# Eight of twelve modulation pieces beside the inverse go to ScalarE and GpSimd, and TensorE sums their partitions

## The reference

```
mod = c_act @ w_ada[l] + b_ada[l]                  # block 1, 6 x 1024 outputs
mod = silu(c) @ ada_w[i, j] + ada_b[i, j]          # block 2, four times 3 x 1024 outputs
q, k, v = causal_conv_silu(h @ w_in ...)           # mixer of block 1
o_dn = chunk_gated_delta_rule(q, k, v, g, beta)    # chunks of 64 tokens, 4 heads
o_sw = sliding_window_attention(...)
x = x + gate1 * (concat(o_dn, o_sw) @ w_out)
```

## Time and profile before

| | |
|---|---|
| median of 3 runs | 2992.44 us (2991.61 to 2999.63) |
| profiled execution, own time | 2987.68 us |
| its span | 2986.0 us |
| mean granted clock of TensorE | 0.961 of full speed |
| busy: TensorE, VectorE, ScalarE, GpSimd | 92%, 38%, 16%, 8% of the span |
| first projection begins | 38 us |
| pieces 20 and 21 | from 258.6 us |
| inverse, slots 0 to 19 | 262.8 to 361.2 us |
| products with k and recurrence | 361.2 to 404.7 us |
| attention | 404.7 to 448 us |
| product with `w_out` | from 451.4 us |

### The profile page before, as it was taken

One profiled execution on the slowest core, in us unless ns is written; L12 is line 12 of the kernel. 1 busy time (PEld: TensorE's weight loads), 2 busy tenths in 40 slices (PEclk: granted clock), 3 DMA queues, 4 the chain that ended last, 5 costly groups with the idle time before them and its releaser, 6 DMA issues.

```text
span 2986.0 us, 37205 instructions
## 1 busy us (share of the span) xinstructions
PE 2748.3 (92%) x15695; PEld 1353.8 (45%) x15695; DVE 1139.2 (38%) x1423; ACT 465.3 (16%) x916; POOL 238.3 (8%) x364
## 2 busy tenths in 40 slices
PE   7988989698899989999995999999999999999998
PEld 3446765232223322232332465477554334546763
DVE  3865453411111111121123254454536663344544
ACT  1122042000000000000000143000013662200001
POOL 1000011011111001101011500000000110000000
PEclk9988989799999999999997999999999999999999
DMA  9776411889999999999999112132223223221310
GB/s 338 282 254 231 179 30 48 315 344 407 401 381 397 409 406 407 409 406 400 413 409 367 38 59 90 57 113 79 90 59 71 58 64 113 106 85 57 112 57 28
DMA packets 170833, 639.49 MB, mean 214 GB/s; under 512 B 75907, under 2 KB 77531, under 8 KB 138129
## 3 DMA queue, kind: packets, MB, share of 16 engines
q1 hardware_dynamic: 156818, 607.76, 53.2%
q0 software_dynamic: 13792, 29.39, 3.4%
q10 hardware_dynamic: 64, 0.07, 0.0%
HBM read 626.44 MB, written 15.23 MB: 215 GB/s over the span
## 4 chain that ended last, share of the span: by engine, by line
PE 50%; issue 33%; DMA 5%; DVE 5%; POOL 3%; POOLq 2%; ACT 2%; DVEq 1%; SPq 0%; ACTq 0%
PE ps L2442 10%; PE ps L2477 10%; PE ps L2780 4%; PE ps L2513 4%; PE ps L2157 3%; DMA slots<-in_ada_w_dram 2%; PE ps L3036 2%; PE ps L2407 2%; PE ps L2324 2%; PE ps L2427 2%; PE ps L1221 2%; POOLq L1677 2%; DMA slots<-in_w_ada_dram 2%; PE ps L2796 1%; POOL work L1686 1%
## 5 line engine op out<-in xcount | busy, mean ns | idle before, releaser
L1787 PE MATMUL ps<-slots,hT 128*32 128x512 f32 x5120 | 564.6, 599 | 13.5 <-DMA slots<-in_w_up_dram 12.4
L1787 PEld LDWEIGHTS ps<-slots,hT 128*32 128x32 f32 x5120 | 165.6, 111 | 387.7 <-issue 365.0
L2477 PE MATMUL ps<-slots,work 128*128 128x512 f32 x672 | 289.6, 592 | 2.8 <-DVE work L2555 2.8
L1825 PE MATMUL ps<-slots,work 128*32 128x512 f32 x2112 | 247.8, 613 | 48.0 <-DMA slots<-in_w_down_dram 46.1
L1939 DVE TENSOR_SCALAR stage<-ps 128x512 f32<-128x512 f32 (+1 forms) x47 | 32.2, 686 | 548.8 <-PE ps L1791 548.4
L2477 PEld LDWEIGHTS ps<-slots,work 128*128 128x128 f32 x672 | 127.5, 190 | 162.5 <-issue 157.8
L2442 PE MATMUL ps<-hT,slots 128*128 128x256 f32 x768 | 168.7, 379 | 0.0
L1825 PEld LDWEIGHTS ps<-slots,work 128*32 128x32 f32 x2112 | 69.9, 112 | 196.3 <-issue 191.0
L2780 PE MATMUL ps<-hT,slots 128*128 128x512 f32 x352 | 156.6, 601 | 0.0
L2442 PEld LDWEIGHTS ps<-hT,slots 128*128 128x128 f32 x768 | 145.9, 190 | 22.4 <-issue 2.9
L2652 DVE TENSOR_TENSOR work<-work,ps 128x1024 f32<-128x1024 f32 x60 | 71.6, 1218 | 165.2 <-PE ps L2477 164.9
(11 more groups left out here) (587 smaller groups left out, 3431.2 us busy)
## 6 DMA issues: line engine op xcount, KB each, us to landing
slots<-in_w_up_dram SPq DMA_DIRECT2D x128, 2048.0 KB, 20.3
slots<-in_w_down_dram SPq DMA_DIRECT2D x64, 2048.0 KB
slots<-in_mlp_w_dram SPq DMA_DIRECT2D x32, 2048.0 KB, 7.9
slots<-in_ada_w_dram SPq DMA_DIRECT2D x40, 1024.0 KB, 4.9
slots<-in_w_ada_dram SPq DMA_DIRECT2D x16, 1024.0 KB, 5.6
slots<-in_w_in_dram SPq DMA_DIRECT2D x5, 2048.0 KB, 15.7
slots<-in_rnn_w_in_dram SPq DMA_DIRECT2D x24, 384.0 KB, 4.2
slots<-in_w_ada_dram SPq DMA_DIRECT2D x4, 2048.0 KB, 12.6
```

Of the source, the lines that this page charges most:

```text
L1787: ins = pe.matmul(to, x[:, k, unit * UNIT:(unit + 1) * UNIT], upw[s][:, k % 2, col:col + CH], start=k == 0, stop=False)
L1825: ins = pe.matmul(to, actT[:, 4 * q + j, 64 * u + 32 * h:64 * u + 32 * h + 32], downw[sl[h]][:, j, half * CH:(half + 1) * CH], start=k == ...
L2477: ins = pe.matmul(ps[:, bank + t], x[:, k, t * P:(t + 1) * P], w[:, k], start=k == 0, stop=k == HK - 1)
```

## The change

Group 5 stays with TensorE, and its pieces now stand ahead of slot 0 (20 and 21), in slot 1 (22) and in slot 2 (23). Groups 6 and 7 become 16 units of 1 MB (128 rows of 2048 columns). SyncE loads them through the two halves of slot 4; unit h waits until unit h - 2 has been summed. ScalarE multiplies a unit in place by its column of `cT` (`pool_scale`), GpSimd adds it to an accumulator in slot 5 in two instructions of 1024 columns (`pool_sum`; for the first unit of a group they are copies), and TensorE sums over the partitions and adds the bias as it does for the side groups: group 6 in slot 18, group 7 behind the recurrence. Which columns belong to groups 5, 6 and 7 is exchanged, and the bias rows are loaded to match. `w_out` is loaded when slot 4 and slot 5 have been read for the last time. The wait for the stored modulations moves from ScalarE to GpSimd. The semaphore `c_silu` is renamed `c_made` and also counts the scaled units.

```diff
+        POOL_FIRST = 6
+        POOL_UNITS = (N_ADA - POOL_FIRST) * KT
+        POOL_BEFORE = 5
...
-            if g < 6:
-                return [(w2v[g - 2], 0, 4 * CH, A2 + (g - 2) * 3 * D)]
-            return [(w2v[l], 4 * CH, HALF, A2 + l * 3 * D + 4 * CH) for l in (2 * (g - 6), 2 * (g - 6) + 1)]
+            if g < 5 or g == 6:
+                l = 3 if g == 6 else g - 2
+                return [(w2v[l], 0, 4 * CH, A2 + l * 3 * D)]
+            return [(w2v[l], 4 * CH, HALF, A2 + l * 3 * D + 4 * CH) for l in ((2, 3) if g == 5 else (0, 1))]
...
@@ ada_bias_loads
-                g.dma_start(dst[2:6], b2v[:, half * D:(half + 1) * D]).then_inc(S("dnw_in"), 16)
-                g.dma_start(dst[6:8], b2v[:, 2 * D:3 * D].rearrange("(g h) n -> g h n", h=2)[:, half]).then_inc(S("dnw_in"), 16)
+                g.dma_start(dst[2:5], b2v[0:3, half * D:(half + 1) * D]).then_inc(S("dnw_in"), 16)
+                g.dma_start(dst[5:6], b2v[2 + half:3 + half, 2 * D:3 * D]).then_inc(S("dnw_in"), 16)
+                g.dma_start(dst[6:7], b2v[3:4, half * D:(half + 1) * D]).then_inc(S("dnw_in"), 16)
+                g.dma_start(dst[7:8], b2v[half:half + 1, 2 * D:3 * D]).then_inc(S("dnw_in"), 16)
...
@@ ada_sp
-            for n in range(N_SIDE, 4 * N_ADA):
+            for n in range(N_SIDE, 4 * POOL_FIRST):
...
+            for h in range(POOL_UNITS):
+                g, k = POOL_FIRST + h // KT, h % KT
+                if h < 2:
+                    sp.wait_ge(freed[4], loads[4])
+                else:
+                    sp.wait_ge(S("side_free"), N_SIDE + h - 1)
+                dst, src = ada_slots[:, 4, h % 2], w2v[3, k * P:(k + 1) * P, 0:4 * CH]
+                if g == 7:
+                    dst, src = dst.rearrange("p (l n) -> p l n", l=2), w2v[0:2, k * P:(k + 1) * P, 4 * CH:4 * CH + HALF].rearrange("l p n -> p l n")
+                sp.dma_start(dst, src).then_inc((landed[4], S("side_in"))[h % 2], 16)
+
+        def pool_part(h):
+            return ada_slots[:, 4, h % 2].rearrange("p (j n) -> p j n", j=4)
+
+        def pool_scale(a, h):
+            k = h % KT
+            if h % 2 == 0:
+                a.wait_ge(landed[4], 16 * (POOL_BEFORE + h // 2 + 1))
+            else:
+                a.wait_ge(S("side_in"), 16 * (N_SIDE + h // 2 + 1))
+            a.activation(pool_part(h), pool_part(h), ACT.Copy, scale=cT[:, 1, k:k + 1]).then_inc(S("c_made"), 1)
+
+        def pool_sum(pool, g):
+            acc = side_acc(g)
+            for k in range(KT):
+                h = (g - POOL_FIRST) * KT + k
+                if h == 0:
+                    pool.wait_ge(freed[5], 4)
+                pool.wait_ge(S("c_made"), 1 + h + 1)
+                for j in (slice(0, 2), slice(2, 4)):
+                    if k == 0:
+                        ins = pool.tensor_copy(acc[:, j], pool_part(h)[:, j])
+                    else:
+                        ins = pool.tensor_tensor(acc[:, j], acc[:, j], pool_part(h)[:, j], ALU.add)
+                ins.then_inc(S("side_free"), 1)
+                pool.drain()
...
@@ side_pe
-            pe.wait_ge(S("side_free"), 4 * (g + 1))
+            if g < POOL_FIRST:
+                pe.wait_ge(S("side_free"), 4 * (g + 1))
+            else:
+                pe.wait_ge(S("side_free"), N_SIDE + KT * (g - POOL_FIRST + 1))
...
@@ dn_pe
                 if i == 10:
                     pe.wait_ge(S("sw_made"), 1)
+                    pe.wait_ge(S("v_out"), TT)
...
-                if N_SIDE + 2 + i < 4 * N_ADA:
-                    ada_pe(pe, N_SIDE + 2 + i)
+                if i in (1, 2):
+                    ada_pe(pe, N_SIDE + 1 + i)
+                if i == 18:
+                    side_pe(pe, POOL_FIRST)
...
+            side_pe(pe, POOL_FIRST + 1)
...
@@ dn_act
-            for g in range(N_SIDE // 4, N_ADA):
-                ada_act(a, g)
+            ada_act(a, N_SIDE // 4)
+            for h in range(4):
+                pool_scale(a, h)
             a.wait_ge(S("sw_made"), 2)
             a.activation(rroot[:, 0:16], rqk[:, 0:16], ACT.Sqrt)
             a.activation(g_s[:, 0:TT * (SH + SG)], g_s[:, 0:TT * (SH + SG)], ACT.Sqrt).then_inc(S("sw_rms"), 1)
+            for h in (4, 5):
+                pool_scale(a, h)
             a.wait_ge(S("sw_turned"), 3)
             a.copy(kTs, ps[:, 4])
             a.copy(kT2, ps[:, 5]).then_inc(S("sw_rms"), 1)
+            for h in range(6, 10):
+                pool_scale(a, h)
+            ada_act(a, POOL_FIRST)
...
                 a.copy(vn[u % 2][r], ps[r, u % 2].rearrange("p (h d) -> p h d", h=DH)).then_inc(S("v_new"), 1)
+                if 10 + n < POOL_UNITS:
+                    pool_scale(a, 10 + n)
...
-            a.wait_ge(S("ada_out0"), 64 * 4)
-            a.wait_ge(S("ada_out1"), 64 * 4)
+            ada_act(a, POOL_FIRST + 1)
...
@@ the program of SyncE
-                pair_sp(sp, A["w_out"][0], 4)
+                sp.wait_ge(S("side_free"), N_SIDE + POOL_UNITS)
+                load(sp, 4, wview(A["w_out"][0, :, 0:CH]))
+                sp.wait_ge(S("ada_done"), N_ADA + 1)
+                load(sp, 5, wview(A["w_out"][0, :, CH:2 * CH]))
...
@@ the program of GpSimd
-                dn_moves(g); end()
+                pool_sum(g, POOL_FIRST)
+                dn_moves(g)
+                pool_sum(g, POOL_FIRST + 1); end()
+                for p in range(2):
+                    g.wait_ge(S(f"ada_out{p}"), 64 * N_ADA // 2)
```

20 lines of the change are left out of this document (12 added, 8 removed).

## The result

| | before | after |
|---|---|---|
| median of 7 runs on one chip | 2996.05 us | 3006.96 us |
| profiled execution, its span | 2987.68, 2986.0 us | 3003.56, 3001.9 us |
| mean granted clock of TensorE | 0.961 | 0.952 |
| `sw_made` 2 (start of VectorE's scalar of slot 11) | 334.64 us | 314.62 us |
| products with k begin | 361.23 us | 357.34 us |

What follows compares the result with a forecast made beforehand. Serial inverse and recurrence bound it, TensorE paying for modulation pieces on the path. Step copy 0 14.4 us sooner, 7.2 given back, 1.0 for squares: -6.1 us, from 2992.44 to 2986.3 us, range 2977 to 3000.

Steps and rivals of the forecast that it cites:

- part 3: Contention of GpSimd's additions with VectorE: 1 us lost in slots 4 to 8 and 2 us in slot 12.
- part 4: ScalarE's order: step copy 0 comes 14.4 us sooner, then scales ahead of the recurrence's step copies give back 7.2 us.
- Part 1: Slots 0 to 10: TensorE loses modulation pieces, biases and waits for weights, -20.3 us, before contention.
- the one wait for weights that was to stay: Slots 0 to 10: of 6.4 us waiting for modulation weights, about 1.0 stays, for piece 22 in slot 1.
- Contention in slots 4 to 8: VectorE's two-input operations beside GpSimd's additions cost 1 us there, after 0.6 us of slack a slot.
- Part 2: Price of a 1 MB unit: load 4.9 us, scale 2.0, GpSimd's sum 4.1, or 2.2 for a copy unit.
- the loop: Load, scale and sum of units through two buffers, forecast to turn in 5.6 us a unit.
- Rival D: GpSimd and VectorE block each other at full length, slot 12 costing 4.1 us; 2991 or 2999 us; chance 0.10.
- Rival C: TensorE's clock falls in the recurrence because it idles 0 to 3 us a step; 3000 to 3010 us; chance 0.16.
- the wait for unit 7: End of slot 18: TensorE arrives at 339.0 and waits until 340.0 for unit 7's sum.
- the 1.0 for the squares: Recurrence: 1.0 us more because `squares(1)` stands behind scale 14 and VectorE waits on it.

Runs made afterwards that it cites:

- early45: The changed kernel with ScalarE scaling units 4 and 5 ahead of the square roots instead of behind them, nothing left out; 2993.01 us, ratio 1.0009 to before.
- skip45: The changed kernel without GpSimd's four additions of units 4 and 5 (signals stay, part of group 6's modulation missing); 2997.59 us, ratio 1.0012 to before.
- both_issue: On top of both, GpSimd's drain behind unit 10 stands ahead of the issue of the attention's bias load instead of behind it; 2983.86 us, ratio 0.9966.
- both: On early45: sums over partitions moved later, scales of units 10 to 15 respaced, bias load behind unit 10, units 6 and 7 scaled earlier; 2986.34 us.

## Why the prediction was wrong

Two terms of the sum were too small and one was missing. Slot 12 was to cost 2 us and cost 6.94 (part 3); the recurrence was to give back 7.2 and gave back 15.6 (part 4); and the lower clock of TensorE ahead of the recurrence, which cost 6.8 us, had no term at all.

**Part 1 held.** `sw_made` 2 was forecast for 315.5 and came at 314.9. The slots are 3.49 us apart, and the one wait for weights that was to stay (1.0) is 1.61. Contention in slots 4 to 8 was priced at 1 us; it is TensorE's wait of 1.62 at 293.93 instead of 0.57, behind a product of VectorE that took 2.65 us: 1.05. (`sw_made` 2 is taken here where ScalarE's square roots begin behind it, at 314.88.)

**Part 2, the price of a unit, held roughly.** Scale 2.0 forecast, 2.00 measured; copy unit 2.2 and 2.02; sum 4.1 and 4.65. With the estimate from the Trainium skill (GPSIMD Engine Reference, Elementwise — side-by-side cycle accounting) it would have been 4.5, nearer. The scales in the recurrence start 5.99 us apart on average (371.98 to 401.93), where the loop was to turn in 5.6.

**Part 3 failed, and with it the forecast.** The step is "2 us in slot 12". Two things were wrong with it. The list of exposed operations had the two products and not the two copies L989 (L1052 now), which cost 4.62 us instead of 0.49, more than both products together lose; they have one input, and the list was drawn up by the number of inputs. And each instruction was given less than one whole addition of wait where it loses up to one: 2.68 us is 0.69 and 1.99. Expected +2.0, measured +6.94. Rival D had this mechanism and gave it 4.1 us in slot 12 and a chance of 0.10. That the additions and the products would meet at all was no accident that could not be foreseen: the square roots hold the scales of 4 and 5 back until `sw_made` 2, and the same event lets VectorE go on to the products. early45 shows that this order was the whole of slot 12's loss.

**The clock had no term.** Rival C had it fall in the recurrence, because TensorE idles a little in each step. It did fall there (0.50 from 376 to 380 us, 0.86 on average), but first ahead of it, in two places: around the wait of 8.62 us in slot 12, and again behind the wait of 1.95 us in slot 18, with 1.00 in between (336 to 344 us). The matmuls up to step copy 0 took 6.8 us longer than in early45. 2.0 of them lie right behind slot 12 (329.70 to 334.40, where before has 342.78 to 345.51), and 4.8 behind slot 18's wait: from the sum over the partitions to the products with k 10.05 us instead of 6.82 (the forecast had 6.9), and from there to step copy 0 7.41 instead of 5.78. Only the 2.0 are shown to come from slot 12. skip45 and early45 both have the short wait in slot 12 and the same one in slot 18 (1.96 and 1.97 us), and behind it their granted clocks differ:

```profile
344.00:348.00 4.00, 4.00 (x21) 2.90 (x14) 0.69 (x1) 1.50 (x2) 0.00 (x0) 0.50 0.47 192
...
344.00:348.00 4.00, 2.35 (x19) 2.05 (x18) 2.23 (x4) 2.47 (x2) 0.00 (x0) 1.00 0.08 27
```

The first is skip45, whose way to the products with k takes 3.1 us longer for it (33.70, 30.60). both_issue's products with k take 5.47 us, though no wait of TensorE in its slots 12 to 19 is longer than 1.68. What decides whether the clock falls stays open.

**Part 4.** The kT copies, forecast for 328.4, came at 334.60; the products with k at 357.34 instead of 346.9; step copy 0 at 364.75 instead of 352.6. These 12.1 us are 4.9 of slot 12's wait beyond the 2, 6.8 of the clock, 1.0 more of the wait for unit 7 (1.95 where 1.0 was forecast), less the 0.6 that `sw_made` 2 came early. The sum over the partitions was priced at 1.9 and took 1.98 in early45.
In the recurrence the mechanism was right: the scale ahead of the next step copy, its wait a DMA's. Its size was not. The seven steps were to take 38.5 us and took 46.82, since the sum is 0.55 us longer, GpSimd stands still for 3.04 us in the drain behind the load of the bias, and the last two steps, which were to take 8.2 us, take 11.90. Their copies wait for TensorE and not for a scale; VectorE's instructions are stretched there (2.14 us for four elements at 400.85, 2.03 for the decay at 404.88), and the granted clock is low in part of the time (0.69 from 404 to 408). Of the 8.3 us, 3.7 lie in the last two steps and 4.6 in the first five; a finer split was not measured. The 6.5 us from step copy 7 to the attention, and that nothing of group 7 adds to them, came as forecast (6.55).
Together: 12.1 + 8.3 = 20.4 late at step copy 7 (391.1 forecast, 411.57 measured), the 1.0 for the squares did not show, and -6.1 became +13.4 at the attention.

## What to carry to other kernels

Work that moves to GpSimd is beside VectorE's at every moment, so draw up the list of VectorE's instructions on the critical chain by what they read and write in SBUF, copies and four-element products too, and give each one whole GpSimd instruction; then cut GpSimd's instructions short, and place them where VectorE works out of PSUM (its additions with one input there kept 0.68 to 0.69 us beside GpSimd's, as at 296.60 and 299.48 us in the changed kernel). Work with a slow loop of its own (load, scale, sum) must not stand ahead of a short step in the same queue unless its data is there already: six units cost 15.6 us with their scales ahead of the step copies, and nothing once these stood where their loads had landed and GpSimd's instructions were short. And where a change gives TensorE a new wait, leave room for more than its length: behind the wait of 8.62 us its matmuls took 2.0 us longer at once, and 4.8 more later whose cause is not settled.

## What the runs showed of the hardware

- VectorE's instructions with both inputs in SBUF are stretched by up to the length of the GpSimd addition beside them, whatever their own length: a product over four elements of 0.17 us took 2.16 beside additions of 128x1024 and at most 1.27 beside additions of 128x512. A copy of 0.25 us took 2.31 beside the former. Cutting its additions in two costs GpSimd 0.28 us a unit (4.65 to 4.93). GpSimd pays too: 5.12 us for a unit in slot 12, 4.65 alone.
- Beside GpSimd's fills, which only write, the two-input products are untouched (0.69 us) and the copies stretched (0.49 to 1.81 for two).
- A GpSimd `drain` behind a load that GpSimd itself issued kept it idle until the load had landed: 3.04 us in the changed kernel and 7.6 in both. In both_issue, where the drain stands ahead of the issue, the next addition followed at once.
- TensorE's granted clock was 0.50 (1.2 GHz) around its wait of 8.62 us and 0.98 to 1.00 ahead of it:

```profile
314.80:324.00 9.20, 5.71 (x48) 5.35 (x48) 7.66 (x8) 4.13 (x4) 6.65 (x3) 0.98 0.11 20
324.00:332.00 8.00, 2.30 (x11) 2.33 (x12) 6.12 (x6) 0.00 (x0) 3.40 (x2) 0.50 0.66 242
332.00:336.00 4.00, 4.00 (x30) 4.00 (x30) 1.79 (x3) 1.40 (x3) 0.00 (x0) 0.77 0.00 0
```
